# Low parts of four units on VectorE, another bank for the first queries, another order around head 7, and stage tiles moved by 128 bytes

## The reference

```python
for l in range(2):
    sh1, sc1, g1, sh2, sc2, g2 = split(silu(c) @ ada_w[l] + ada_b[l], 6)
    h = rms_norm(x, norm_mix_g[l]) * (1 + sc1) + sh1
    y = stick_window_mixer(h) if l == 0 else hgrn2_mixer(h)
    x = x + g1 * y
    h = rms_norm(x, norm_ffn_g[l]) * (1 + sc2) + sh2
    x = x + g2 * (gelu(conv3(h @ w_gate) + b) * (h @ w_up)) @ w_down
return rms_norm(x, final_g)

def stick_window_mixer(h):                        # layer 0
    sq, sk, sv, wq, wk, wv = split(h @ w_in)      # widths 512 512 512 512 128 128
    # 8 stick-breaking heads of 64: z = q k / 8, strictly causal,
    #   weights = exp(log_sigmoid(z) + sum over later keys of log_sigmoid(-z)), o = weights @ v
    # 8 sliding-window heads over 2 key heads: softmax with ALiBi and a sink, window of 2 chunks of 64
    return concat(o_sb, o_sw) @ w_out
```

## Time and profile before

| what | us |
|---|---|
| median of 3 runs (1384.05 to 1384.78) | 1384.71 |
| the profiled execution, whole | 1383.8 |
| its span, first to last instruction | 1381.9 |
| TensorE busy (matmuls) | 1334.5, 97% |
| VectorE busy | 811.6, 59% |
| ScalarE busy | 561.5, 41% |
| GpSimd busy | 57.4, 4% |

### The profile page before, as it was taken

How to read it: one execution, slowest core, us unless ns; L and a number is a source line. 1 busy time by engine, 2 the same in 40 slices (tenths; PEclk the granted TensorE clock), 3 DMA queues, 4 the chain that set the end, 5 groups by cost and what they waited for, 6 DMA issues and landing times.

```text
span 1381.9 us, 17367 instructions
## 1 busy us (share of the span) xinstructions
PE 1334.5 (97%) x6251; PEld 1085.1 (79%) x6251; DVE 811.6 (59%) x1188; ACT 561.5 (41%) x840; POOL 57.4 (4%) x96
## 2 busy tenths in 40 slices
PE   6899998899999999999999999999999999999998
PEld 5677776686888888888868888887778888888785
DVE  5755447567665666445678777775765545552323
ACT  6465554334333333212155555553343333332213
POOL 2200000000000000000100000000000000000000
PEclk9999998999999999999999999999999999999999
DMA  9343341063455445455722222223523333332222
GB/s 348 112 141 95 104 137 46 1 184 89 141 149 150 137 143 146 143 178 174 236 78 77 76 64 75 62 76 106 169 77 91 95 103 91 96 101 92 89 94 76
DMA packets 191684, 160.38 MB, mean 116 GB/s; under 512 B 5271, under 2 KB 165224, under 8 KB 191634
## 3 DMA queue, kind: packets, MB, share of 16 engines
q1 hardware_dynamic: 179376, 116.87, 27.9%
...
q10 hardware_dynamic: 402, 0.16, 0.0%
...
## 4 chain that ended last, share of the span: by engine, by line
PE 90%; DVE 6%; ACT 3%; issue 1%; DMA 0%; POOL 0%; DVEq 0%; ACTq 0%; POOLq 0%
PE proj L1554 60%; PE z L1554 22%; PE obank L1554 3%; PE misc L1554 3%; DVE ada_sum L1100 1%; DVE w_lo L1005 1%; DVE soft L1192 0%; DVE normed L1038 0%; DMA rstd<-ffn_conv_b 0%; DVE hT_lo L1044 0%; ACT w_hi L618 0%; PE z L2048 0%; ACT q_sb L738 0%; DVE xT L1369 0%; PE z L2026 0%
## 5 line engine op out<-in xcount | busy, mean ns | idle before, releaser
L1554 PE MATMUL proj<-hT_hi,w_hi 128*128 128x512 f32 x1112 | 441.9, 398 | 7.0 <-DVE hT_lo L1044 3.6
L1005 DVE TENSOR_TENSOR w_lo<-w_raw,w_hi 128x1024 fp32r<-128x1024 f32 x189 | 231.2, 1224 | 347.6 <-ACT w_hi L618 347.6
L1554 PE MATMUL proj<-hT_lo,w_hi 128*128 128x512 f32 x1112 | 434.1, 390 | 1.3 <-DVE hT_lo L1128 1.3
L1554 PE MATMUL proj<-hT_hi,w_lo 128*128 128x512 f32 x1112 | 434.2, 391 | 0.0
L618 ACT ACTIVATE w_hi<-w_raw 128x1024 fp32r<-128x1024 f32 x191 | 202.2, 1060 | 453.2 <-PE proj L1554 266.0
L1554 PEld LDWEIGHTS proj<-hT_hi,w_hi 128*128 128x128 f32 x1112 | 209.4, 188 | 58.7 <-DVE hT_lo L1044 6.8
L1554 PEld LDWEIGHTS proj<-hT_lo,w_hi 128*128 128x128 f32 x1112 | 209.5, 189 | 45.2 <-DVE hT_lo L1128 1.7
L1554 PEld LDWEIGHTS proj<-hT_hi,w_lo 128*128 128x128 f32 x1112 | 209.4, 188 | 44.4
L1554 PE MATMUL z<-gated_hi,w_hi 128*128 (+1 forms) x264 | 105.7, 400 | 0.1
L1554 PE MATMUL z<-gated_hi,w_lo 128*128 (+1 forms) x264 | 104.2, 395 | 0.0
L1554 PE MATMUL z<-gated_lo,w_hi 128*128 (+1 forms) x264 | 104.2, 395 | 0.0
...
## 6 DMA issues: line engine op xcount, KB each, us to landing
...
ada_first<-ada_w SPq DMA_DIRECT2D x16, 512.0 KB, 10.6
...
```

Of the source, the lines that this page charges most:

```text
L1005: nc.vector.tensor_tensor(w_lo[:, slot, :], w_raw[:, slot, :], w_hi[:, slot, :].bitcast(F32), ALU.subtract).then_inc(lo_done, 1)
L1554: return nc.tensor.matmul(dst, weights_ap, moving, start=start, stop=stop, skip_group_check=True)
```

## The change

Six things are edited. (1) GpSimd's four subtractions go; `quad_split(u)` does them on VectorE, two in the first half of the start and two after the second half's last block. (2) `quad_banks` is turned by one: SQ gets `zb[0]`, WK gets `obank`; the wait for WK's copies moves from head 0's scores to head 0's values. Four `keep_clock` matmuls are added before the second half of the quad. (3) VectorE clears one pair of key tiles before the quad's end and the three others behind the copies of WK. (4) Unit WQ+1 leaves head 2, WQ+2 and WQ+1 each move back one place, and WQ+3 stands in head 7 between scores and sums; the scores of window heads 0 and 1 stand between B and C of head 7; VectorE's split for the second output unit moves behind `window_max(2)`, and `HEAD_BLOCKS` and the order of VectorE's window work follow. (5) In the last round of the window heads `window_values(6)` and two steps of the output pair stand ahead of `window_transposes(7)`, and two more steps behind it. (6) A tile of 128 bytes a partition, `stage_pad`, is put behind `c_now`; nothing reads or writes it.

```diff
@@ -73,12 +73,12 @@
 STEPS0 = [
     ("Q", 0), ("A", 0), ("T", 0), ("u", WV), ("B", 0), ("u", SQ + 1), ("T", 4), ("C", 0),
     ("A", 1), ("u", SK + 1), ("B", 1), ("u", SV + 1), ("C", 1),
-    ("A", 2), ("T", 1), ("u", WQ), ("B", 2), ("u", WQ + 1), ("C", 2),
+    ("A", 2), ("T", 1), ("u", WQ), ("B", 2), ("C", 2),
     ("A", 3), ("u", SQ + 2), ("B", 3), ("u", SK + 2), ("C", 3),
-    ("A", 4), ("u", SV + 2), ("B", 4), ("T", 2), ("u", WQ + 2), ("C", 4),
+    ("A", 4), ("u", SV + 2), ("B", 4), ("T", 2), ("u", WQ + 1), ("C", 4),
     ("A", 5), ("u", SQ + 3), ("B", 5), ("u", SK + 3), ("C", 5),
-    ("A", 6), ("u", SV + 3), ("B", 6), ("T", 3), ("u", WQ + 3), ("C", 6),
-    ("A", 7), ("L", 0), ("B", 7), ("C", 7),
+    ("A", 6), ("u", SV + 3), ("B", 6), ("T", 3), ("u", WQ + 2), ("C", 6),
+    ("A", 7), ("u", WQ + 3), ("B", 7), ("L", 0), ("L", 1), ("C", 7),
 ]
 UNITS0 = QUAD + [b for kind, b in STEPS0 if kind == "u"]
 HALVES0 = DC // 2
@@ -101,7 +101,7 @@
 MOD_FROM = 3
 GAP_MODS = {2: (9, 10), 3: (11,)}
 MOD_COLUMNS = [(), (), (), (0, 1), (2, 3), (4, 5), (6,), (7,)]
-HEAD_BLOCKS = [2, 2, 2, 2, 2, 2, 3, 3]
+HEAD_BLOCKS = [2, 2, 2, 2, 2, 3, 3, 2]
 
 
 MISC = (
@@ -194,6 +194,8 @@
         cond = sb("cond", [P, 3, DC])
         lower = sb("lower", [P, 3, DC])
         c_now = sb("c_now", [P, LINE])
+
+        sb("stage_pad", [P, 2 * LINE])
 
 
         table2 = h32[:].rearrange("p a n -> p (a n)")[:, 0:7 * P]
@@ -273,7 +275,7 @@
 
         x_banks = [zb[1 + dc % 3] for dc in range(DC)]
         unit_banks = [zb[0], zb[1], zb[2], zb[3], proj[0], proj[1], obank, zb[0]]
-        quad_banks = [proj[0], proj[1], obank, zb[0]]
+        quad_banks = [zb[0], proj[0], proj[1], obank]
 
         out_banks = [proj[0], proj[1], zb[2], zb[3]]
         down_banks = [[zb[0], zb[1], zb[2], zb[3]], [proj[0], proj[1], zb[0], zb[1]]]
@@ -573,11 +575,6 @@
             pool.dma_start(sinks[:, 0:SW_HEADS], ab_sinks.partition_broadcast(P).rearrange("p a h -> p (a h)")
                            ).then_inc(const_in, 16)
 
-            for u in range(len(QUAD)):
-                pool.wait_ge(hi_done, u + 1)
-                hi, lo = (w_hi[:, u, :], w_lo[:, u, :]) if u < 2 else (quad_hi[u % 2], quad_lo[u % 2])
-                nc.gpsimd.tensor_tensor(lo, w_raw[:, u % 2, :], hi.bitcast(F32), ALU.subtract).then_inc(quad_low, 1)
-
             pool.wait_ge(unit_mm, len(QUAD))
             for j in range(2 * DC, 11 * DC):
                 load(j)
@@ -728,9 +725,9 @@
             def window_exp(h):
                 s = h % 3
                 act.wait_ge(max_done, h + 1)
-                if h in (1, 2):
+                if h == 2:
                     act.wait_ge(pv_done, SB_HEADS)
-                elif h:
+                elif h > 2:
 
                     act.wait_ge(pt_full, 2 * h - 4)
                 for b in range(TB):
@@ -811,7 +808,7 @@
                         nc.scalar.activation(weights[:, Z_OFF[j]:Z_OFF[j] + Z_LEN[j]], zb[j][:, 0:Z_LEN[j]],
                                              ACT.Exp).then_inc(wt_done, 1)
                 elif kind == "L":
-                    window_exp(0)
+                    window_exp(b)
                 elif kind == "T":
                     act.wait_ge(misc_full, MISC_AT[f"V{b}"] + 1)
                     nc.scalar.activation(v_nat0[:, :, b * P:(b + 1) * P],
@@ -819,7 +816,6 @@
                                          ).then_inc(misc_free, 1)
 
 
-            window_exp(1)
             window_copy(0)
             window_exp(2)
             for h in range(1, SW_HEADS):
@@ -1005,6 +1001,11 @@
                 nc.vector.tensor_tensor(w_lo[:, slot, :], w_raw[:, slot, :], w_hi[:, slot, :].bitcast(F32),
                                         ALU.subtract).then_inc(lo_done, 1)
 
+            def quad_split(u):
+                dve.wait_ge(hi_done, u + 1)
+                hi, lo = (w_hi[:, u, :], w_lo[:, u, :]) if u < 2 else (quad_hi[u % 2], quad_lo[u % 2])
+                nc.vector.tensor_tensor(lo, w_raw[:, u % 2, :], hi.bitcast(F32), ALU.subtract).then_inc(quad_low, 1)
+
             def split_first(u):
 
                 dve.wait_ge(half_hi, BEHIND_PAIR[u])
@@ -1155,16 +1156,20 @@
                 first_block(0, i)
             dve.wait_ge(misc_free, MISC_AT["small"] + 1)
             nc.vector.tensor_tensor(lower[:, 0, :], gamma[0], gamma[1], ALU.subtract).then_inc(small_ready, 1)
+            quad_split(0)
             first_columns(0)
             first_low(0)
+            quad_split(1)
             first_block(1, 0)
             for dc in range(1, HALVES0):
                 first_low(dc)
                 first_block(1, dc)
             for i in range(HALVES0, DC):
                 first_block(1, i)
+            quad_split(2)
             first_columns(1)
             first_low(HALVES0)
+            quad_split(3)
             for dc in range(HALVES0 + 1, DC):
                 first_low(dc)
             dve.wait_ge(lower_exp, 1)
@@ -1175,9 +1180,12 @@
             dve.wait_ge(bands_in, 16)
             link(nc.vector.tensor_copy(table_r[:], table2))
             dve.wait_ge(xt_full, DC)
-            for hp in range(4):
-                nc.vector.memset(k_sb[HEAD:P, hp, :], 0.0).then_inc(k_clear, 1)
-                nc.vector.memset(k_odd[hp][0:HEAD, :], 0.0).then_inc(k_clear, 1)
+            def clear_keys(pairs_of_heads):
+                for hp in pairs_of_heads:
+                    nc.vector.memset(k_sb[HEAD:P, hp, :], 0.0).then_inc(k_clear, 1)
+                    nc.vector.memset(k_odd[hp][0:HEAD, :], 0.0).then_inc(k_clear, 1)
+
+            clear_keys(range(0, 1))
 
             def clear_queries():
                 for hp in range(4):
@@ -1228,8 +1236,10 @@
                             last = nc.vector.tensor_copy(k_sw[HEAD * half:HEAD * half + HEAD, g, :],
                                                          quad_banks[3][HEAD * g:HEAD * g + HEAD, :])
                     last.then_inc(quad_out[3], 1)
+                    clear_keys(range(1, 4))
                 elif kind == "u":
-                    split(u + 2, u % 2)
+                    if b != WQ + 3:
+                        split(u + 2, u % 2)
                     if b >= WQ:
                         dve.wait_ge(unit_mm, u + 1)
                         src = proj[u % 2]
@@ -1243,6 +1253,8 @@
                                                     ALU.mult)
                             nc.vector.tensor_scalar(q_odd[hp][HEAD:P, :], src[HEAD:P, :], HEAD ** -0.5, None,
                                                     ALU.mult).then_inc(proj_free[u % 2], 1)
+                    if b == WQ + 3:
+                        ada_blocks(HEAD_BLOCKS[SB_HEADS - 1])
                     if b in MOD_IN_UNIT0:
                         mod_group(MOD_IN_UNIT0[b])
                     u += 1
@@ -1265,19 +1277,18 @@
                 elif kind == "B" and b == 0:
                     clear_queries()
                 elif kind == "L":
-                    window_max(0)
-                    ada_blocks(1)
-                    window_norm(0)
-                    ada_blocks(HEAD_BLOCKS[SB_HEADS - 1] - 1)
+                    window_max(b)
+                    if b:
+                        window_norm(0)
                 elif kind == "C" and b % 2:
                     dve.wait_ge(pv_done, b + 1)
                     nc.vector.tensor_copy(oT0[:, b // 2, :], obank[:]).then_inc(o_free, 1)
 
 
-            window_max(1)
+            window_norm(1)
             window_max(2)
+            split(U_OUT0 + 1, 1)
             window_copy(0)
-            window_norm(1)
             for h in range(1, SW_HEADS):
                 window_copy(h)
                 if h + 1 < SW_HEADS:
@@ -1740,6 +1751,8 @@
             misc_wait("first1")
             first_sums(1)
             x_columns(range(6, DC))
+            pe.wait_ge(x_new, 6)
+            keep_clock(zb[3], 4)
 
             def tile_in(b):
 
@@ -1803,7 +1816,7 @@
                     quad(1)
                 elif kind == "u":
                     if u < len(QUAD) + 2:
-                        tile_in(QUAD[u % 2])
+                        tile_in(QUAD[1 + u % 2])
                     else:
                         pe.wait_ge(proj_free[u % 2], (u - len(QUAD)) // 2)
                     unit(u, u % 2, proj[u % 2][:], mod_group=MOD_IN_UNIT0.get(b))
@@ -1825,13 +1838,13 @@
                             pe.wait_ge(wt_done, 4 * (b - 1) + i + 1)
                         elif j:
                             pe.wait_ge(x_new, DC)
-                        else:
-                            tile_in(WK)
                         mm(zb[j][:, 0:Z_LEN[j]], sb_keys(b)[:, j * P:(j + 1) * P], q_sb[:, hp, j * P:SEQ],
                            start=True)
                         mm(zb[j][:, 0:P], ident_r[:], strict_r, stop=True).then_inc(z_full, 1)
                 elif kind == "L":
-                    window_logits(0)
+                    if b:
+                        pe.wait_ge(wt_done, 4 * SB_HEADS)
+                    window_logits(b)
```

(24 more changed lines are left out.)

## The result

The changed kernel takes **1361.55 us** (median of 4 runs, 1360.34 to 1362.0) where the kernel before takes 1384.38 us (4 runs beside them on the same chip, 1383.42 to 1384.78). The ratio is 0.9835, with a 95% interval from 0.9818 to 0.9852. That is 22.8 us less, where 25.1 were forecast. The profiled execution of the changed kernel took 1361.85 us, its span is 1360.0 us; before it was 1381.9.

What follows compares the result with a forecast made beforehand. TensorE, busy for 97% of the span, was taken as the bound. Terms -7.5 - 2.8 + 0.4 + 0.8 - 8.8 + 0.5 - 7.7 = -25.1 us bring 1384.7 to 1359.6 us, range 1355.5 to 1369.

Steps and rivals of the forecast that it cites:

- the three stretched terms: Start, VectorE: a scaling, a four-column scaling and five accumulations lose 1.95, 1.1 and 3.9 us beside GpSimd; these 6.9 us go.
- split 0: Start: the first subtraction moved to VectorE lies in its wait for the column sums and costs 0.25 us.
- TensorE is then idle for about 1 us: Start, before the second half's column sums: TensorE's wait for VectorE's last accumulation shrinks from 3.94 us to about 1 us.
- I take the clock as kept: Start: column sums take 1.95 us, 1.6 us less; transposes and the first eight matmuls behind them another 0.9 us less.
- the clearings as a cost only, +0.4 us: Head 0: six clearings behind WK's copies delay the softplus sum that the cumulation waits for, +0.4 us (0 to 0.7).
- +0.8 at head 2: Head 2 loses the unit between cumulation and values, so the exponential shows as a wait: +0.8 us (0.6 to 1.2).
- the slow clock of head 7: Head 7: with its waits gone, the cumulation takes 2.6 us less and the values 1.8 us less.
- The new wait: Before window head 0's values, TensorE waits for VectorE's queued work: 2.4 us (1 to 4), with full-speed durations behind it.
- rival (b): Clock falls behind window head 1's transposes, or later VectorE splits delay the start: about 5 us lost, 1364.6 us; 10%.
- Its price of 0.0059 us a matmul: Down-projections and layer 1's output projection: the pad saves 0.0059 us on each of 1248 matmuls, 7.4 us.
- Rival (a): Down-projections, output projection and quad: the pad does nothing, taking 7.7 us from the gain, 1367.3 us; 14%.
- Rival (c): Down-projections and output projection: the moving operand's new place is worse, pace over 0.247 us, kernel slower; 1401 us at 0.26; 3%.

## Why the forecast came out as it did

The forecast of 1359.6 us was 2 us too low, within its range; between the two profiled executions, on which its steps are priced, it was 3.2 us too low. Each row of the table came out with the sign forecast. By its steps:

**Part 1 (-7.5, measured -6.3 in the traces without the pad's 0.3, and -5.3 by experiment).** The mechanism is shown: with the subtractions back on GpSimd the same VectorE instructions are stretched again, and the three stretched terms came out at 1.12, 1.95 and 3.94 us in the traces of before and after. The column sums started at 41.68 and not at 40.5, 1.2 us late, and that is the whole miss. 0.8 us of it is the last accumulation, which ended at 41.23 and not at 40.45. Of that, 0.36 us is no step of the prediction: in this execution all of the start runs later by as much (the seven first accumulations begin at 14.18, in the earlier trace rows at 13.82). Some 0.3 us is split 0, priced at 0.25 us, which holds up `scale_g` by 0.55: it waits until 25.24 for ScalarE's high part. The other 0.4 us is TensorE. "TensorE is then idle for about 1 us" and "I take the clock as kept" looked only behind the sums, and the prediction did not work out when TensorE would be ready for them. Behind the sums the clock is kept, and the 1.6 us are there: 3.57 less 1.84. But it is at its lower level near 30 us, in the quad's first half, where before it wasn't, and that half ends at 40.37 + 1.47 with its transposes. So TensorE itself is late and does not wait for the sum at all. In the execution of the kernel with the output copy moved the clock did not fall there:

```profile
40.84 1.95 PE L1567 MATMUL misc<-table,ada_sum 128*128 128x1 f32 x16 [0.58 <-DVE ada_sum L1101]
```

There TensorE waits for 0.58 us and starts 0.06 us behind the last accumulation. Why the clock falls in one and not in the other isn't settled; the two kernels are alike up to there.

**Parts 2 and 3 (-2.4, measured -2.95).** The sum was near but the shares were wrong, which the old banks showed. The banks give 1.2 us and the clearings 1.7, where 2.8 and a loss of 0.4 were forecast: two errors that nearly cancel, so the near sum is luck. The prediction had the clearings as a cost only, +0.4 us, because it looked at what is queued behind them in their new place and not at what was queued behind them in the old one. The cost didn't come: VectorE ends the clearings at 62.40 + 0.48 = 62.88, and the first cumulation starts at 64.85, right at the end of the unit ahead of it. These are the rows of after that show it:

```profile
62.40 0.48 DVE L1186 MEMSET square<- 64x512 f32 x1 [0.16 <-issue]
62.91 1.68 DVE L1266 SCALAR_TENSOR_TENSOR soft_a<-z,soft_a 128x128 f32<-128x128 f32 x4
```

**Part 4 (-8.8 at head 7 and behind, measured -6.7; +0.8 at head 2, measured +0.9).** All the waits that were to go went, and so did the slow clock of head 7. The old order of heads brought them back. The new wait was sized at 2.4 us and is 2.63. The step that failed is the sentence that full-speed durations would stand behind it, because they did behind the 2.53 us of the earlier trace rows. In the profiled execution the clock fell, and values 0 to values 1 took 1.6 us more than in two executions with the same wait in which it didn't. That is rival (b), at one of the two places that it named, and it accounts for 1.6 of the 2.1 us. The prediction had a row for a wait of this length with the clock kept, and none with it fallen. The rest, 0.5 us, is of the size of three small terms together: the new wait is 0.2 us longer, head 7's values gave 1.6 us and not 1.8, and 0.3 us of wait are left before transposes 1.

**Part 5 (+0.5).** The traces of before and after and the trace with the part undone both show +0.5 us; the times alone can't.

**Part 6 (-7.7, measured -7.8 alone and -5.7 when taken out).** The tiles that would gain and the size were right. Its price of 0.0059 us a matmul came from counting records in a window; from start to start it is 0.2324 - 0.2269 = 0.0055 in all long stretches but one, which gives 6.9 us for the 1248 matmuls, as the last row of the table has it. Whether the place of one operand or its distance to the other sets the pace is open. Rival (a) is refuted by the pad alone, and so is the outcome that follows from the Trainium skill's cache lines. The Trainium skill (SBUF — State Buffer, Specifications (TRN2)) gives 16-byte lines; the shifts tried here are 64 and 128 bytes, whole numbers of such lines, and the pace of a matmul changed with both. Rival (c), a pace over 0.247 us, did not appear at any place tried; the slowest is 0.2334.

By the experiments' ratios the parts sum to 5.7 (pad) + 5.3 (subtractions) + 9.3 (parts 4 and 5) + 1.9 (banks) = 22.2 us, by the medians to 18.2. Each of these terms has 2 to 3 us of its own uncertainty, so that the sum comes near the whole of 22.8 us proves little. The clearings' 1.7 us are not in it: they were not undone by themselves, and the figure is what is left of 2.95 us after the banks.
